# A two-layer decoder trunk on one core: where the second layer's expert operands lie, and the order of the lower-half products

## The reference, cut to what matters

```python
def block_fn(xb):                      # xb: normalised tokens
    q = (xb @ w_q).reshape(PEER_BLOCK, PEER_HEADS, D_QUERY)
    s1 = einsum(q[..., :D_HALF], k1);  s2 = einsum(q[..., D_HALF:], k2)
    ...                                # top 16 of 16 x 16 pairs for each of 8 heads
    eid = e1 * N_KEYS + e2             # one of 16384 experts
    g = softmax(ts)
    a = gelu(einsum('thkd,td->thk', u_tab[eid], xb))
    return einsum('thk,thkd->td', g * a, v_tab[eid])
```

## Time and profile before

| | us |
|---|---|
| median of three runs | 2256.3 |
| the profiled execution | 2254.77 |
| its span, first to last instruction | 2253.1 |
| TensorE (PE) busy in the span | 2231.6 (99%) |
| VectorE (DVE) busy | 1706.2 (76%) |
| ScalarE (ACT) busy | 1353.1 (60%) |
| GpSimd (POOL) busy | 854.6 (38%) |

### The profile page before, as it was taken

How to read it: one execution, slowest core, us unless ns; L and a number is a source line. 1 busy time by engine, 2 the same in 40 slices (tenths; PEclk the granted TensorE clock), 3 DMA queues, 4 the chain that set the end, 5 groups by cost and what they waited for, 6 DMA issues and landing times.

```text
span 2253.1 us, 49289 instructions
## 1 busy us (share of the span) xinstructions
PE 2231.6 (99%) x15792; PEld 2088.5 (93%) x15792; DVE 1706.2 (76%) x3283; ACT 1353.1 (60%) x2705; POOL 854.6 (38%) x766
## 2 busy tenths in 40 slices
PE   8999999999999999999999999999999999999998
PEld 8999999999999888888999999999999998888887
DVE  6556769966888788788874567699488878878887
ACT  6544546667777555555764545566677775555555
POOL 3100108988777122121121001299877761111110
PEclk9999999999999999999999999999999999999999
DMA  6545455555444899888554455455554458888884
GB/s 222 162 142 168 167 175 167 186 180 185 158 158 157 267 309 324 268 306 287 170 192 159 144 168 184 140 186 186 186 172 156 157 181 276 299 306 270 291 273 137
DMA packets 127141, 462.94 MB, mean 205 GB/s; under 512 B 14704, under 2 KB 14864, under 8 KB 126288
## 3 DMA queue, kind: packets, MB, share of 16 engines
q1 hardware_dynamic: 106416, 385.20, 49.1%
q0 software_dynamic: 20640, 76.68, 12.0%
HBM read 457.87 MB, written 3.95 MB: 205 GB/s over the span
## 4 chain that ended last, share of the span: by engine, by line
PE 97%; DVE 2%; issue 1%; ACT 0%; POOLq 0%; POOL 0%; DVEq 0%; ACTq 0%
PE ps L1435 21%; PE ps L1440 20%; PE ps L1436 20%; PE ps L1673 10%; PE ps L1674 10%; PE ps L1675 10%; PE ps L1629 1%; PE ps L1630 1%; PE ps L1588 1%; PE ps L1551 0%; POOLq L323 0%; DVE w_lo L874 0%; DVE h_lo L913 0%; PE ps L1553 0%; PE ps L1534 0%
## 5 line engine op out<-in xcount | busy, mean ns | idle before, releaser
L397 POOL TENSOR_TENSOR w_lo<-raw,w_hi 128x512 fp32r<-128x512 f32 x508 | 645.0, 1292 | 256.6 <-ACT w_hi L498 159.2
L1435 PE MATMUL ps<-h_hi,w_hi 128*128 128x256 f32 (+1 forms) x2592 | 653.9, 289 | 10.2 <-DVE h_lo L855 8.0
L1436 PE MATMUL ps<-h_lo,w_hi 128*128 128x256 f32 (+1 forms) x2592 | 641.7, 283 | 0.0
L1435 PEld LDWEIGHTS ps<-h_hi,w_hi 128*128 128x128 f32 x2592 | 489.4, 189 | 11.6 <-issue 9.5
L1436 PEld LDWEIGHTS ps<-h_lo,w_hi 128*128 128x128 f32 x2592 | 489.8, 189 | 0.2
L476 ACT ACTIVATE w_hi<-raw 128x1024 fp32r<-128x1024 f32 x334 | 351.6, 1053 | 190.6 <-PE ps L1440 189.7
L1243 DVE TENSOR_TENSOR w_lo<-raw,w_hi 128x512 fp32r<-128x512 f32 x504 | 347.7, 690 | 126.5 <-ACT w_hi L724 85.2
L1674 PE MATMUL ps<-w_lo,h_hi 128*128 128x512 f32 x1016 | 398.5, 392 | 0.0
L1675 PE MATMUL ps<-w_hi,h_lo 128*128 128x512 f32 x1016 | 398.5, 392 | 0.0
L1673 PE MATMUL ps<-w_hi,h_hi 128*128 128x512 f32 x1016 | 398.5, 392 | 0.0
L874 DVE TENSOR_TENSOR w_lo<-raw,w_hi 128x1024 fp32r<-128x1024 f32 x208 | 256.5, 1233 | 186.6 <-ACT w_hi L476 185.5
(11 more groups left out here) (225 smaller groups left out, 2971.0 us busy)
## 6 DMA issues: line engine op xcount, KB each, us to landing
raw<-stream SPq DMA_DIRECT2D x730, 512.0 KB, 3.4
bias<-bias_in POOLq DMA_DIRECT2D x2, 1152.0 KB, 6.8
x_keep<-x POOLq DMA_DIRECT2D x2, 1152.0 KB, 5.3
x<-x_keep POOLq DMA_DIRECT2D x2, 1152.0 KB, 9.6
x<-x_in SPq DMA_DIRECT2D x4, 288.0 KB, 5.3
y_out<-t_op SPq DMA_DIRECT2D x4, 288.0 KB, 2.1
ws<-ws_in POOLq DMA_DIRECT2D x2, 512.0 KB, 4.2
ring<-u_rows,rows POOLq DMA_INDIRECT x44, 5.9
```

The source lines that it names most:

```text
L397: return pool.tensor_tensor(w_lo[:, k % 2, lo_col:hi_col], raw[:, k, lo_col:hi_col], w_hi[:, k % 2, lo_col:hi_col].bitcast(F32), ALU.subtract)
L1435: pe.matmul(out, wh, rhs_hi, start=first, stop=False)
L1436: pe.matmul(out, wh, rhs_lo, start=False, stop=False)
```

## The change

`spaced` is called with start 0 for both layers, and the order of the lower-half products of the first expert stage becomes 0, 2, 1, 3, 4, 6, 5, 7 in both layers, in both loops of that stage. The first four still use the first half of `w_lo` and the last four the second half, so the waits stand where they stood. The chunks are sums into the same PSUM place, whatever their order.

```diff
+PAIRED = [0, 2, 1, 3, 4, 6, 5, 7]
...
-        prompt_hi = [spaced(h_hi, 0, 288, C), spaced(h_hi, 8, 288, C)]
-        prompt_lo = [spaced(h_lo, 0, 288, C), spaced(h_lo, 8, 288, C)]
-        mixed_hi = [spaced(h_hi, 0, 256, 4), spaced(h_hi, 8, 256, 4)]
-        mixed_lo = [spaced(h_lo, 0, 256, 4), spaced(h_lo, 8, 256, 4)]
+        prompt_hi = [spaced(h_hi, 0, 288, C), spaced(h_hi, 0, 288, C)]
+        prompt_lo = [spaced(h_lo, 0, 288, C), spaced(h_lo, 0, 288, C)]
+        mixed_hi = [spaced(h_hi, 0, 256, 4), spaced(h_hi, 0, 256, 4)]
+        mixed_lo = [spaced(h_lo, 0, 256, 4), spaced(h_lo, 0, 256, 4)]
...
                             pe.wait_ge(lo_half, L * LOWS + i * 4 + (j + 1))
-                            for c in range(C // 2):
+                            for c in PAIRED[0:C // 2]:
                                 m = with_lower(out, j, c * P, prompt_hi[L][c], False)
                             m.then_inc(mm_half, 1)
                             pe.wait_ge(lo, u0 + i * 4 + (4 * Q_U + j + 1))
-                            for c in range(C // 2, C):
+                            for c in PAIRED[C // 2:C]:
                                 m = with_lower(out, j, c * P, prompt_hi[L][c], c == C - 1)
                             m.then_inc(mm, 1)
...
-                            m = with_lower(out, j, c * P, prompt_hi[L][c], c == C - 1)
+                            m = with_lower(out, j, PAIRED[c] * P, prompt_hi[L][PAIRED[c]], c == C - 1)
```

## The result

The changed kernel takes 2239.89 us (median of 4 runs, 2239.02 to 2240.83) against 2255.71 us for the kernel before in the same comparison (4 runs, 2254.97 to 2257.0). The ratio is 0.9932, with a 95% interval of 0.9920 to 0.9944: 15.8 us less, where 15.1 were forecast. The forecast in time was 2241.2 us; 0.6 of the 1.3 us that it lies too high is the kernel before, whose median was 2256.3 in three runs and is 2255.71 in these four. The span of the profiled execution falls from 2253.1 to 2237.3 us.

A forecast was written before the change was run, and what follows sets the result against it. TensorE's matmul spacing was taken to bound the kernel; 10.3 + 1.6 + 3.2 = 15.1 us less than the profiled 2254.77 gave 2239.7, or 2241.2 as a median of runs, with 8 in 10 from 2237.5 to 2247.0.

The forecast's parts named there:

- What bounds: Whole kernel: TensorE is busy 99% of the span, so time lies in matmul spacing; its waits should stay at 12 us.
- Placement in the second stage: Second expert stage, second layer: operands moved to offset 0 shorten 127 units by 80.8 ns each, 10.3 us less.
- the placement is not the cause: Rival: something else slows the second layer's matmuls and stays, the order gives nothing either; 2256.3 us, chance 0.04.
- Placement in the first stage: First expert stage, second layer: unit falls from 2.826 to 2.814 us, 12 ns over 128 units, 1.6 us less.
- The order: First expert stage, both layers: seven lower-product steps go from 118.5 to 116.7 ns, 12.6 ns a unit, 3.2 us less.
- What hides the rest: Other engines and routing beside the expert stages: GpSimd and VectorE still fit the shorter units, so nothing else becomes late.

## Why the prediction was right

- *What bounds.* Distances on TensorE and no waits: shown. The busy time fell by 15.1 us. The waits went from 12.4 to 11.6 us, which was not forecast; 0.7 of it, the wait for `ext`, is luck as far as the runs show, for in the kernels of the experiments it was anything up to 1.5 us.
- *Placement in the second stage.* Forecast 127 x 80.8 ns, measured 80: shown, and by the placement alone. The rival that the placement is not the cause falls with that run. The Trainium skill's rule ("TensorE: Matmul & The Clock Gate", "Step-by-step: what each phase is for") that loading weights takes nothing from the running matmul cannot be all there is: the same products take 226.7 or 233.3 ns by where the stationary operand lies. Another rival was not named: that other engines and transfers, which use the same memory, hold TensorE up. It was not tested by itself. That 125 of 127 unit distances agree to the ns, and that eight shifts gave the same four values in both layers, speaks against it.
- *Placement in the first stage.* Forecast 1.6 us, from a unit 12 ns shorter; the placement alone took it from 2.826 to 2.814. The same 12 ns were put down for the mixing loop without a row; there the placement alone took the second layer's unit from 3.346 to 3.333, so it held.
- *The order.* Forecast 12.6 ns a unit in each layer, measured 14 against the 2.814 of order 0 to 7, and as much in the mixing loop: 3.6 us in place of 3.2, which is within the reading. The value of the upper products was the right row to take, and the reason given for it (two of a kind in a row) held in the other orders with the operands at 0. As a general rule it was not enough: it gave the wrong values once the lower activations or `w_lo` were moved alone, so that the change kept all operands at 0 was part of why it came out.
- *What hides the rest.* One size was off without cost. VectorE's wait for the exponentials, its slack in the earlier trace rows, was to shrink by 2.0 us and shrank from 12.9 to 8.6. Counted from the first product of the stage, the exponentials came 0.7 us sooner in the first layer and 1.4 in the second, close to the forecast; the rest is VectorE's own chain, which ended 1.1 us later in either layer. In the first layer that chain ended some 143.6 us after this product before, with the placement alone and in the kernel with `b` moved, and 144.8 us after it in the changed kernel and with the order alone. Why was not tried. Row of the changed kernel:

```profile
DVE total L1143 <- ACT route L670: 8.6, 2, 4.5
```

- *What stays open.* Why the low 8 bits matter. Parity of neighbours accounts for the paired and unpaired orders with all operands at one shift, but rows of four or eight of a kind, operands all at 128, and lower activations or `w_lo` moved alone came out otherwise than a fixed price for each step would have it.

## What to carry to other kernels

When TensorE is busy without waits and two loops of the same shape run at different spacings, compare the addresses of their stationary and moving operands in the low 8 bits; a loop in the same trace whose operands lie alike is the control. Then test an order only together with a placement, since the order that helped at one placement cost as much at another. Distances read from first start, last start and count resolve a few ns, far below what timed runs of 2250 us can tell. All of this was seen with operands of 4 bytes in one kernel; whether other types behave so was not tried.

## What the runs showed that was not expected

- The spacing of a matmul is not set by its columns alone: 512 columns took 226.7 to 233.3 ns and 256 columns 116.7 to 120 on average, by where the operands lay and in which order they came, at a granted clock of 1.00 and without waits.
- In the second expert stage the spacing repeats when the stationary operand is moved by 256 bytes, 16 bytes changed nothing, and 32, 64 and 128 bytes of one shift cost the same 78 to 80 ns in a unit of 12.
- Chunks all at phase 0 (1024 bytes apart) were the slowest layout of the first stage, 2.880 us, all at 128 took 2.846, and 128 bytes more a chunk, two of a kind in a row, was the fastest, 2.800.
- A product's spacing goes by more than its own operands: with `w_lo` moved, the next six steps of the upper products changed, though they read none of it.
